# Reordering the projections, attention steps and modulation loads of the first block of a fused two-block transformer kernel

## What is computed

```python
h = x @ w_in                                    # 1024 x 9216
ua, va, za, qh, kh, vh, zb, ga, gb = split(h)
ua = gelu(ua); va = layer_norm(gelu(va))
ya = ua * (tril(w_s) @ va + b_s) * silu(za)     # 8 groups, chunks of 128
q, k = rope(qh) * dk**-0.5, rope(kh)
o = softmax(q0 k0) v - lam * softmax(q1 k1) v   # 8 heads, causal
yb = rms_norm(o) * silu(zb)
merged = sigmoid(ga) * (ya @ w_a) + sigmoid(gb) * (yb @ w_b)
ple = sigmoid(x @ w_pg) * (p @ w_ple)
x = layer_norm(ALPHA * x + merged @ w_out + ple)
```

## Time and profile before

| | |
|---|---|
| three executions | 1174.40, 1176.03, 1178.73 us |
| profiled execution | 1178.73 us, span 1177.0 us |
| mean granted TensorE clock | 0.965 of full |
| TensorE busy, matmuls | 1087.6 us (92%) |
| TensorE busy, weight loads | 707.6 us (60%) |
| VectorE, ScalarE, GpSimd busy | 507.4, 396.7, 28.4 us |
| moved by DMA | 320.65 MB, mean 272 GB/s |

### The profile page before, as it was taken

How to read it: one execution, slowest core, us unless ns; L and a number is a source line. 1 busy time by engine, 2 the same in 40 slices (tenths; PEclk the granted TensorE clock), 3 DMA queues, 4 the chain that set the end, 5 groups by cost and what they waited for, 6 DMA issues and landing times. The chain is left out here.

```text
span 1177.0 us, 13027 instructions
## 1 busy us (share of the span) xinstructions
PE 1087.6 (92%) x5182; PEld 707.6 (60%) x5182; DVE 507.4 (43%) x988; ACT 396.7 (34%) x680; POOL 28.4 (2%) x81
## 2 busy tenths in 40 slices
PE   6999899989899787799997999999999999999994
PEld 4877677868677675687874844535353535353542
DVE  5835456563765675545563412222222222222213
ACT  4533656464533352547543211111111111111112
POOL 1000000000000000000000000000000000000000
PEclk9999998999999989899998899999999999999997
DMA  9665525475656435255347859999999999999990
GB/s 331 192 230 185 209 74 210 172 258 189 248 181 233 138 126 166 88 176 179 107 141 265 332 235 393 412 417 417 417 417 417 417 417 417 417 417 417 418 384 37
DMA packets 93933, 320.65 MB, mean 272 GB/s; under 512 B 6288, under 2 KB 7328, under 8 KB 76976
## 3 DMA queue, kind: packets, MB, share of 16 engines
q1 hardware_dynamic: 92256, 315.02, 70.3%
q0 software_dynamic: 752, 3.22, 0.8%
q10 hardware_dynamic: 864, 1.57, 0.4%
HBM read 318.74 MB, written 1.05 MB: 272 GB/s over the span
## 5 line engine op out<-in xcount | busy, mean ns | idle before, releaser
L734 PE MATMUL ps<-hl,L 128*128 128x512 f32 (+1 forms) x1216 | 387.3, 400 | 14.6 <-DVE rlo L1504 10.7
L734 PEld LDWEIGHTS ps<-hl,L 128*128 128x128 f32 x1216 | 229.6, 192 | 72.7 <-issue 24.5
L1504 DVE TENSOR_TENSOR rlo<-ring,hl 128x1024 fp32r<-128x1024 f32 (+1 forms) x154 | 185.0, 1217 | 178.4 <-ACT hl L1153 177.5
L734 PE MATMUL ps<-rlo,L 128*128 128x512 f32 (+1 forms) x608 | 239.9, 395 | 0.0
L1153 ACT ACTIVATE hl<-ring 128x1024 fp32r<-128x1024 f32 (+1 forms) x154 | 159.3, 1054 | 204.9 <-DMA ring<-in_w_in 98.2
L734 PE MATMUL ps<-slots_all,xe 128*64 128x512 f32 (+1 forms) x1056 | 226.9, 582 | 0.8 <-DVE rt L2241 0.8
L734 PEld LDWEIGHTS ps<-slots_all,xe 128*64 128x64 f32 x1056 | 73.9, 137 | 131.7 <-issue 128.5
L734 PEld LDWEIGHTS ps<-rlo,L 128*128 128x128 f32 x608 | 116.6, 192 | 25.0
L734 PE MATMUL ps<-slots_all,hh 128*64 128x512 f32 x512 | 115.6, 593 | 0.0
L1510 DVE SCALAR_TENSOR_TENSOR hh<-ps,gslot,hh 128x256 f32<-128x256 f32 x32 | 15.5, 483 | 191.2 <-ACT hh L1153 191.2
L1153 ACT ACTIVATE hh<-ps 128x256 f32<-128x256 f32 x64 | 24.7, 386 | 207.4 <-PE ps L734 196.7
(11 more groups left out here) (209 smaller groups left out, 785.9 us busy)
## 6 DMA issues: line engine op xcount, KB each, us to landing
slots_all<-in_w_exp_gate SPq DMA_DIRECT2D x64, 1024.0 KB, 20.1
slots_all<-in_w_exp_up SPq DMA_DIRECT2D x64, 1024.0 KB, 16.2
slots_all<-in_w_exp_down SPq DMA_DIRECT2D x64, 1024.0 KB, 16.8
ring<-in_w_in SPq DMA_DIRECT2D x49, 1024.0 KB, 7.1
ring<-in_w_mod SPq DMA_DIRECT2D x24, 1024.0 KB, 5.2
ring<-in_w_out SPq DMA_DIRECT2D x8, 1024.0 KB, 5.3
ring<-in_w_ple_gate SPq DMA_DIRECT2D x4, 1024.0 KB, 5.4
ring<-in_w_branch_a SPq DMA_DIRECT2D x4, 1024.0 KB, 6.9
```

The costliest lines, as they stand in the source:

```text
L734: return e.matmul(o, l, r, start=start, stop=stop)
L1504: return e.tensor_tensor(o, a, b, op)
```

## The change

The change alters the order of the first part and moves some loads. The matmuls, their shapes and their number stay.

- The blocks run v, q, k, za, ua, va, gb, zb, ga, pg, ple ... in place of q, k, v, za, ua, va, zb, gb, ga, pg, ple ... kT stands behind za0 in both, qT behind k1 (before: behind v0).
- SP issues the xT loads first, then three weight loads, then the constants in another order, then the rest. The first load isn't split. x is split into high and low parts whole, ahead of v0.
- Two head steps in each of za1, ua0, ua1, va0 and va1, where there was one in each of ten blocks.
- The mod pairs go in the order 0 to 11. m4 and m5 move from g0 and g2 to gb0 and zb1; m6 and m7 to ga0 and pg0; m8, m9 and m10 from ple0, bb0 and behind wp1 to fv, g0 and g2. Only m11 is left behind wp1.
- The bgate load moves from behind `yb_set` to the start; zb's buffer is B(4) for gbuf; ga, gb and pl use other buffers; the head norm's squares go to UA and its job starts in ga0 (before: pg0). wsT is loaded beside aln. The turn ybT stands ahead of ple0.
- `idle` jobs on ScalarE: generators that yield and issue no instruction.

```diff
-        UA, VA, ZB, GA, GB, ZG, PL, R, XN = B(2), B(6), B(0), B(3), B(6), gbuf, B(5), B(0), B(1)
+        UA, VA, ZB, GA, GB, ZG, PL, R, XN = B(2), B(6), B(0), B(5), B(3), B(4), B(6), B(0), B(1)
...
-        for name in ("q0 q1 k0 k1 m0 v0 v1 m1 za0 za1 m2 ua0 ua1 m3 va0 va1 aln zb0 ws zb1 gb0 m6 gb1 m7 ga0 ga1 "
-                     "pg0 pg1 m8 ple ba0 ba1 m9 bb0 bb1 wo0 wo1 ln c0 fq up fk fv m4 g0 g1 m5 g2 g3 om0 om1 "
-                     "of0 of1 wp0 wp1 m10 m11").split():
+        for name in ("v0 v1 q0 q1 m0 k0 k1 m1 za0 za1 m2 ua0 ua1 m3 va0 va1 m4 aln gb0 gb1 zb0 m5 zb1 m6 ga0 m7 ga1 "
+                     "pg0 pg1 ple ba0 ba1 bb0 bb1 wo0 wo1 ln c0 fq up fk m8 fv m9 g0 g1 m10 g2 g3 om0 om1 "
+                     "of0 of1 wp0 wp1 m11").split():
...
-        MOD_IN = {"v1": [0], "za1": [1], "ua1": [2], "va1": [3], "gb1": [6], "ga0": [7], "ple0": [8], "bb0": [9],
-                  "g0": [4], "g2": [5]}
+        MOD_IN = {"k1": [0], "za1": [1], "ua1": [2], "va1": [3], "gb0": [4], "zb1": [5], "ga0": [6], "pg0": [7],
+                  "fv": [8], "g0": [9], "g2": [10]}
...
-        MOD_LATE = [10, 11]
+        MOD_LATE = [11]
...
-        HEADS_IN = {name: (s,) for s, name in enumerate("za1 ua0 ua1 va0 va1 zb0 zb1 gb0 gb1 ga0".split())}
+        HEADS_IN = {"za1": (0, 1), "ua0": (2, 3), "ua1": (4, 5), "va0": (6, 7), "va1": (8, 9)}
...
-        AFTER = {"v0": "qT", "za0": "kT", "gb1": "yaT", "ple1": "ybT", "bb1": "mT", "of1": "mT2"}
+        AFTER = {"k1": "qT", "za0": "kT", "zb1": "yaT", "pg1": "ybT", "bb1": "mT", "of1": "mT2"}
...
         @block.sync
         def _(e):
             w = Waits(e)
+            for q in range(4):
+                e.dma_start(XTF[:, 2 * q:2 * q + 2, :], D["xT"][:, 2 * q:2 * q + 2]).then_inc(xt_in[q], 16)
+
...
             for i, (kind, parts) in enumerate(loads):
+                if i == 3:
+                    for n, (dst, src) in enumerate(consts):
+                        e.dma_start(dst, src).then_inc(consts_in, 16)
                 if i >= NS:
                     freed(i - NS)
-                if i == 0:
-                    src = parts[0][2]
-                    for q, s in enumerate((first_in, slot_sem[0])):
-                        e.dma_start(slot(0)[:, 1024 * q:1024 * q + 1024].rearrange("p (a b) -> p a b", a=2),
-                                    src[:, 2 * q:2 * q + 2]).then_inc(s, 16)
-                    continue
...
         @block.gpsimd
         def _(e):
             w = Waits(e)
-            for dst, src in consts:
-                e.dma_start(dst, src).then_inc(consts_in, 16)
+            w.wait_ge(x_lo, 4)
+            e.dma_start(gbuf[:, :, :], bass.AP(D["bgate"].tensor, 0, [[0, 128], [1024, 2], [1, 1024]])).then_inc(gb_in, 16)
...
             def head_norm():
+                aux_done(("yaT", 1, 4))
                 w.wait_ge(*read(("o", 7)))
-                oo, sq_ = OO.rearrange("p m n -> p (m n)"), KT.rearrange("p m n -> p (m n)")
+                oo, sq_ = OO.rearrange("p m n -> p (m n)"), UA.rearrange("p m n -> p (m n)")
...
             w.wait_ge(ones_set, 1)
             act(st[:, 255:256], ones[:, 0:1], ACT.Copy)
+            for q in range(4):
+                w.wait_ge(xt_in[q], 16)
+                act(L0[:, 0, 2 * q:2 * q + 2, :], XTF[:, 2 * q:2 * q + 2, :], ACT.Copy).then_inc(x_hi, 1)
+            project("v0", into(VV, 0))
             job = side.add(set_up())
+            project("v1", into(VV, 1))
             project("q0", into(RAW, 0))
             project("q1", into(RAW, 1))
             side.finish(job)
+            job = side.add(idle(12))
             w.wait_ge(x_lo, 4)
             project("k0", into(KRAW, 0))
+            side.finish(job)
             project("k1", into(KRAW, 1))
-            project("v0", into(VV, 0))
             turned("qT", QTF)
-            project("v1", into(VV, 1))
```

More of the change, by code:

```diff
@@ L207, in two_blocks @@
         GTV = st[:, 112:240].rearrange("p (m e) -> p m e", m=2)
-        loads, pieces, blocks, mods, once = [], [], {}, {}, {}
+        loads, pieces, blocks, mods, once = [], [], {}, [], {}
         WI, W2 = D["w_in"], D["w_in_2"]
@@ L242, in two_blocks @@
                 c = int(name[1:])
-                mods[c] = [load("mod", (slice(0, 2048), 4, kn(D["w_mod"], 512 * c, 512 * c + 512)[:, k0:k0 + 4]))
-                           for k0 in (0, 4)]
+                mods.append([load("mod", (slice(0, 2048), 4, kn(D["w_mod"], 512 * c, 512 * c + 512)[:, k0:k0 + 4]))
+                             for k0 in (0, 4)])
             elif kind in FIRST:
@@ L429, in two_blocks @@
             if name in AFTER:
-                aux_turn(AFTER[name], "va" if name in ("v0", "za0") else "v")
-            if name == "zb1":
+                aux_turn(AFTER[name], "va" if name in ("k1", "za0") else "v")
+            if name == "gb0":
                 for m in range(2):
@@ L531, in freed_by @@
             if kind == "mod":
-                c = next(q for q in mods if i in mods[q])
+                c = [i in pair for pair in mods].index(True)
                 return next((blocks[name][0] for name in MOD_IN if c in MOD_IN[name]), npieces)
-            after = {"aln": "zb0", "wsT": "zb1", "pT": "pg0", "ln": "wo1", "qup": "fq", "kvup": "fq"}[kind]
+            after = {"aln": "gb0", "wsT": "gb0", "pT": "ga1", "ln": "wo1", "qup": "fq", "kvup": "fq"}[kind]
             return blocks[after][-1] + 1
@@ L899, in h_ready @@
                 w.wait_ge(h_lo, 2 * (kk // 4) + m + 1)
-            for name in ("q0", "q1", "k0", "k1", "v0"):
+            for name in ("v0", "v1", "q0", "q1", "k0", "k1"):
                 project(name, L0, x_ready)
             turn("qT", lambda m, j: ROT[:, m, 128 * j:128 * j + 128], lambda m, j0: w.wait_ge(roped, 2))
-            for name in ("v1", "za0"):
-                project(name, L0, x_ready)
+            project("za0", L0, x_ready)
             turn("kT", lambda m, j: ROT[:, m, 128 * j:128 * j + 128], lambda m, j0: w.wait_ge(roped, 4))
-            for name in ("za1", "ua0", "ua1", "va0", "va1", "zb0", "zb1"):
+            for name in ("za1", "ua0", "ua1", "va0", "va1", "gb0"):
                 project(name, L0, x_ready)
@@ L918, in _ @@
                     taken(x)
-            for name in ("gb0", "gb1"):
+            for name in ("gb1", "zb0", "zb1"):
                 project(name, L0, x_ready)
@@ L1170, in mod_part, with idle @@
                 aux_done(("mp", c))
-                if c in before_mod:
-                    aux_done(("mod", before_mod[c]))
+                if c > 1:
+                    aux_done(("mod", c - 2))
                 act(macc[:, c % 2, :], bank(("mp", c))[:, :], ACT.Copy, scale=1.0 / 32).then_inc(aux_a.sem, 1)
+            def idle(n):
+                for _ in range(n):
+                    yield
             def set_up():
@@ L1821, in _ @@
             e.memset(ones[:, :], 1.0).then_inc(ones_set, 1)
+            for q in range(4):
+                s = slice(2 * q, 2 * q + 2)
+                w.wait_ge(x_hi, q + 1)
+                tt(L0[:, 1, s, :], XTF[:, s, :], L0[:, 0, s, :].bitcast(F32), ALU.subtract).then_inc(x_lo, 1)
+            project("v0")
             job = side.add(set_up())
-            project("q0")
-            project("q1")
+            for name in ("v1", "q0", "q1"):
+                project(name)
             side.finish(job)
@@ L1865, in _ @@
                 tt(UA[:, m, :], UA[:, m, :], ZB[:, m, :], ALU.mult).then_inc(ya_set, 1)
-            for name in ("gb0", "gb1"):
+            for name in ("gb1", "zb0", "zb1"):
                 project(name)
             completed("yaT")
+            job = side.add(head_norm())
             for name in ("ga0", "ga1"):
                 project(name)
-            job = side.add(head_norm())
-            project("pg0")
             w.wait_ge(p_hi, 1)
@@ L1875, in _ @@
                 .then_inc(p_lo, 1)
-            project("pg1")
+            for name in ("pg0", "pg1"):
+                project(name)
+            side.finish(job)
+            completed("ybT")
             def ple(c):
```

72 lines of the change are left out of this document (25 added, 47 removed).

## The result

Seven executions of each kernel on one chip: the kernel before 1175.21 us (1173.23 to 1178.73), the changed kernel 1184.13 us (1180.65 to 1187.78), ratio 1.0074, 95% interval 1.0052 to 1.0096. The change makes the kernel 8.9 us slower. That lies inside the predicted range of 1166 to 1191 us, but the likeliest case, no difference at 1177 us, was not what happened; "slower by over 0.5%" was, to which the prediction gave 0.36.

The account below looks back on a forecast made before the run. TensorE, busy 92% of the span, was taken as the bound, with its waits and half clock in the dense part deciding. Terms summed to -0.6, with 2 put back +1.4, giving 1177 us against the 1176.03 median; range 1166 to 1191.

Parts of the forecast that it names:

- Start, +0.4: Kernel start: first matmul later at 11.6 us, later gaps in q0 gone, net +0.4 us, bounds -2 and +3.
- kT, +5.4: kT transposes: wait of 6.5 us for k's rope plus 3.0 of clock, less waits gone; net +5.4, bounds -4 and +9.
- if kT has none: Sign against the forecast: no wait of over 3 us at kT, where 5 to 8 us was expected near 100 us.
- Two heads a block, +8.4 and -3.9: za1: wait 5.4 plus 3.0 clock, +8.4; ua1 unchanged; va1's 2.75 plus 3.0 gone, gb0 waits 1.9, net -3.9.
- Rival A: Paired heads stall again and again: ua1 and va1 also get za1's wait and clock loss, 1188 to 1191 us; chance 0.26.
- Gates and branches, -3.1, +0.7, -2.9: Waits beside mod pairs 6 and 7 gone, -3.1; head norm delays ga0 and pg0, +0.7; wait at 321.29 gone, -2.9.
- the 2.0 put back: Allowance of 2 us for small waits under 1 us that the new order would have and could not be listed.
- fk and fv, -1.9, +0: Rest of the latents' rope starts 1.9 us earlier, -1.9; m8 in fv finds no wait, +0 to +3.
- End, -3.7: Dense part's end: m10 ahead of g2, one mod pair left after wp1, gate sum 3.7 us earlier; bounds -4 and 0.
- Rival D: Clock stays low between waits at kT, za1 and ua1, +10 us each, 1197 us; chance 0.06.
- Rival C: The last mod pair was hidden: the root waits for something else, the -3.7 goes, 1181 us; chance 0.12.

Follow-up runs that it names:

- b_vfirst: The kernel before with only v0 and v1 ahead of q and k, m0 used in k1, qT behind k1: 1182.97 us, ratio 1.0044.
- a_m8bb: The changed kernel with modulation pair 8 back in bb0 and none in fv: 1185.94 us, ratio 1.0093.
- a_sum8: The changed kernel with the sum of modulation product 8 made at the start of g1 instead of g0: 1183.92 us, ratio 1.0058.
- b_m9fv: The kernel before with modulation product 9 moved from bb0 to fv, its sum in g1: 1174.24 us, ratio 0.9970.

## Why the prediction was right in range and wrong in its middle

The five parts measured alone come to +7.6 (heads), +5.2 (v first), +2.3 (start), -3.5 (a pair to fv) and -3.2 (one late pair fewer), together +8.4 us, where the whole measures +8.9. Part of this agreement is luck. Each part has an interval of some 3 us to each side, so the sum has about 6, and the parts are not quite those of the change: the 5.49 of the paired heads alone has no counterpart in the changed kernel, the moves of products 9 and 10 stand for others in it, and the gates and buffers were not run alone.

*Start, +0.4.* Right within what can be told. The first matmul was forecast at 11 to 12 us and came at 12.54; v0 was to be done by 25, and v1's first matmul starts at 24.96.

*kT, +5.4.* The size agrees (5.2 measured alone, interval 2.5 to 7.9), the place does not. The prediction let TensorE pass `mod_sum` in 1.0 us and wait 6.5 at kT. In fact it stopped already at that sum, for q's bank, and reached kT as rope ended. By the prediction's own sign ("if kT has none") the step is wrong: the profile has 0.61 us there. The run with that sum taken away has the wait where it was forecast, 7.24 us. Both are VectorE's in-order list with k's rope at its end.

*Two heads a block, +8.4 and -3.9.* Single rows are right: 5.77 for the 5.4 in za1, 4.86 for the 5.2 in ua1, none in va1, 2.56 for the 1.9 in gb0. But the sum was too low. Together with the two gate waits taken off (-3.1) the paired heads were forecast at +1.4 net, and alone they measure +7.6. In the kernel before, the 3.1 was not won but turned into the 5.49 behind yaT. That row is absent in the changed kernel, where the turn and product 6 stand elsewhere, and gb0's 1.49 and 2.56 stand instead; what the pairing costs inside the changed kernel no run measures. Rival A, which priced stalls that pass on from block to block at 1188, had the sign of it, but not the mechanism: ua0, va0 and va1 have no wait.

*Gates and branches, -3.1, +0.7, -2.9.* The waits went, as forecast; none over 1 us is left in the first profile from 230 us on, one of 1.81 in the second. In sum the first part was forecast at +5.0 and the 2.0 put back made 7.0; it measures +5.5 in the second profile, and -0.1 in the first, where no stretch from 200 to 400 us fell to half clock. With the profiles that repeat the first parts it is about +4.

*fk and fv, -1.9, +0.* **This is the step that failed**, "m8 is used in fv, where the burst is two loads: no wait found". The gain in front was larger than forecast: to the km transposes 6.8 us for the 1.9. Behind it stands what the step did not see. ScalarE's and TensorE's rows of the changed kernel; first ScalarE:

```profile
481.09 2.01 ACT L1143 ACTIVATE hl<-ring 128x1024 fp32r<-128x1024 f32 x2 [7.43 <-DMA ring<-in_w_in]
...
493.33 0.37 ACT L1143 ACTIVATE ex<-ps,st 128x128 f32<-128x128 f32 x1 [2.37 <-DVE st L1503]
```

g0's load comes late behind m8 and m9, ScalarE stands 7.43 us at it, the second pair's exponentials come after, and the next user of a PSUM bank, the sum at 494.30, waits 3.85. There is also more work: one product more than before (1.92 us), and two sums of 16 one-column matmuls where one sum of two wide ones stood (2.08 us each for 1.08). And the clock is at 1.2 GHz over parts of 492 to 502 and 520 to 528 us, 2.6 and 3.4 us lost by the windows above. From km to the sum of g2's pair that is 12.5 us more: 3.1 of standing still, 6.0 of clock and 3.3 of the rest. With pair 8 back at bb0 the same stretch is only 2.8 us longer than before, so nearly all of it hangs on that move. The prediction had put the 1.7 of a moved sum at 0 on the ground that it only changed its place, and counted the product in fv at 0 unless it had to wait.

*End, -3.7.* Half of a sum. The stretch behind mT2 is 3.65 us shorter in the changed kernel and in the run of this move alone. But a pair that leaves the end arrives elsewhere. In the run alone 1.7 us are paid for it ahead of mT2, so the term is -2.0 there. In the changed kernel three products stand between the layer norm and mT2 where two stood, and the third is the one in fv, whose price is in the 12.5 above. The step counted what left one place and not what arrived in the other.

*The sum.* The first part came out near its forecast; the second, forecast at -5.6 to -2.6, came out at +3.6 in one profile and +3.9 in the other. The four profiles with the changed kernel's second part agree (228.9 to 229.2 us, against 224.4 to 226.8 in four of the five with the old one). That miss of 6 to 9.5 us covers the whole distance between 1177 and 1184, and the first part's miss goes the other way. Rival D (a clock that stays low between the waits at 90, 131 and 169 us) did not happen; a window of the changed kernel between the first two:

```profile
98.00:130.00 32.00, 27.04 (x142) 20.65 (x140) 14.16 (x22) 11.02 (x20) 0.00 (x0) 0.97 0.54 197
```

From 144 to 168 us the granted clock is 0.95. The rule cited from the Trainium skill (TensorE: Matmul & The Clock Gate, HAM oscillation), by which the ramp is paid once for each wait, fits these three waits. It does not fit the rest: in the first profile the wait of 2.56 at 229.01 has no half clock behind it, and 520 to 528 us has half clock with no wait over 0.87 us ahead of it. Rival C was wrong as well, the tail did shorten.

What stays open: what holds up the rest of the wait at q's bank once the loads are thinner and why b_vfirst is at half clock so long behind the layer norm.

## What to carry to other kernels

When work is moved between two places, write down both: what the old place gives back and what the new place pays. Here the end of the dense part gave back 3.65 us and of0 took 1.7: the sum, in a stretch without a hole, cost its full length, and the product only what didn't fit into a hole of 1.07 us that was there before.

When engines run fixed lists, a wait belongs to the slowest chain behind it and not to the instruction that shows it. Taking away the waiting instruction, or letting it wait for less, moved the wait on to the next one twice here (7.24 us for 5.78, and 3.27 for 3.85).

Two profiles of one program differed by 7.5 us of span. Before a gain of 0.5% is read from a trace, the lengths of the waits are to be compared apart from the stretches at half clock.

## What the hardware showed that was not expected

The half clock does not need a long wait. In the second profile of the changed kernel it falls three times between 228 and 300 us: behind a wait of 2.56 us, behind one of 1.81, and behind 16 one-column matmuls with 0.47 us of idle ahead of them. In the first profile the wait of 2.56 stands at the same place (229.01) and the clock stays at 2.4 GHz for the 200 us around it.

What a fall costs doesn't follow the length of the wait either. The three cost 1.4 to 1.7 us each. Behind the wait of 5.78 it is 3.4 us (86 to 98 us: 8.0 busy us, granted 0.57). In the second profile the same place, with a wait of 5.46, costs 2.0.

One fall with no wait over 0.9 us ahead of it comes back from profile to profile. Behind the 16 one-column matmuls of product 9's sum (520.20 in the changed kernel) the clock falls in both profiles of the changed kernel, in a_m8bb, in a_sum8 and in b_m9fv. It costs 3.4 us in the first and 1.7 in each of the other four.
